# Issuing the NSA scores of a hybrid decoder layer inside the following dense product, one core of Trainium2

## The chip, the cores and the metric

One Trainium2 chip, one of its NeuronCores. The time is microseconds on the device for one execution of the whole layer. A run is compared by the median of its executions; the profile is of one further execution. The engines that matter here are TensorE (matmuls), VectorE, ScalarE and the queue of SyncE (SP), which issues the weight loads.

## What is computed

One decoder layer for 512 tokens of width 1024, in fp32. Three attention branches (MLA, a sparse attention "DSA", and NSA) run on one normed input, are gated and merged; cross-attention and an MLP follow. The change is in NSA, whose part of the reference is, shortened:

```python
p_c = masked_softmax(jnp.einsum('btghd,bcgd->bghtc', q, k_cmp) * scale, cmask)
o_c = jnp.einsum('bghtc,bcgd->btghd', p_c.astype(v_cmp.dtype), v_cmp)
...
s = jnp.einsum('btghd,bgtkd->bghtk', qb, kg) * scale + jnp.transpose(bias, (0, 1, 4, 2, 3))
p = masked_softmax(s, (dist >= 0)[:, :, None]).astype(vg.dtype)
o_s = jnp.einsum('bghtk,bgtkd->btghd', p, vg)
...
o = gt[:, :, 0] * o_c + gt[:, :, 1] * o_s + gt[:, :, 2] * o_w
```

There are 8 heads in 2 groups, 31 compressed keys, and, as every block is selected and the window spans the sequence, two causal attentions of 512 keys for each head (o_s and o_w, each with its own keys and values).

## The kernel before

The program gives each engine one list of instructions, and they meet through semaphores. Every list is in order, so a wait holds all that stands behind it on its engine.

**Dense products.** Weights come in slabs of 1 MB, numbered in one order. SP loads slab s into a raw buffer of two once slab s-2 has been split; ScalarE's `high(s)` copies it to its high part once the product that used that place (s-2) is done; VectorE's `low(s)` forms the low part. A product such as `features("nq", p)` is `t_mode` (L660 to L662 inside): 8 chunks of 6 matmuls of 512 columns, three for each of two output banks. `t_mode` calls a function `wait_chunk(k)` ahead of each chunk, where other work can be placed. Results stand in two PSUM pairs that alternate; `free(g)` waits for the one before the last to be taken.

**NSA by pairs.** The 8 heads are done in 4 pairs p. The slabs come in the order nq0, kk0, vv0, nq1, nq2, kk1, vv1, nq3 (nq: queries of a pair, kk and vv: keys and values of a group, two pairs each; compress weights lie between the first of them), and then bg20, bp20, bg21, bp21 and so on: branch gate and branch projection of the third merge. A pair has four causal units u = 2h + w (head h, kind w) and a compressed part for each head.

- Scores, TensorE (L773 in `score_tile`): 4 tiles a unit, of 128, 256, 384 and 512 columns, then two compressed tiles (L1035, four matmuls of 31 columns in each). They go through three PSUM buffers, `SCORE[n % 3]`; a tile waits until the tile three before it has been taken (`score_taken`). Two of these buffers also hold turned tiles, and one an output of the values.
- Softmax: VectorE adds the bias strip and finds the row maximum (`softmax_in`, L1893), ScalarE does the exp (`exps`, L1368), VectorE scales the row by gate over sum (`normalise`, L1904 to L1911). The compressed part has its own steps (L2055 to L2060, then L2071 to L2077).
- Values, TensorE: `attention` returns `begin(n)`, which turns the n-th block of probabilities (L783), and `finish()`, which runs value matmuls (L790), each followed by the turning two blocks on. ScalarE copies each turned block to SBUF (`turned_begin` for the first two, `turned` for the rest; the copy is L1268); a value matmul waits for its copy. At a head's end ScalarE and VectorE (`head_low`, L1916) take the output.

The order on TensorE in `block.tensor`: scores(0); product nq1; values(0); scores(1); product nq2; product kk1; values(1); product vv1; scores(2); product nq3; values(2); scores(3); product bg20; values(3); product bp20. `ahead(begin, KD)` places the first two turned blocks of the values in the last two chunks of the product before them. In `merge(2)` ScalarE applies the sigmoid (L1433) to bg20's result.

VectorE for a pair: takes all 16 score tiles, then the two compressed tiles, then one `low`, then the four `normalise`, then the compressed normalising. It does `low` for slab nq2 ahead of scores(0) and `head_low` of the pair before ahead of the scores. ScalarE for a pair: `turned_begin` of the last pair, query copy (`nsa_query`), `turned`, `high`, then four `exps` and the compressed exps; for pair 2 `high` stands ahead of `turned_begin`. POOL loads the next bias strips once all 18 score tiles of a pair are taken.

Of the kernel before, what the change touches and what calls it, by code (L numbers as in the profile page):

```python
# [81 lines left out]
def layer(nc, a, out):  # L82
# [11 lines left out]
    with ctx:  # L94
# [552 lines left out]
        def _(pe):  # L647
# [233 lines left out]
            def merge(b, last_values, after=lambda name, n: None):  # L881

                begin, finish = last_values
                for n in range(GROUPS):
                    g = product_at["bg", b, n]
                    free(g)
                    t_mode(slab_at["bg", b, n], two(g), both, KD, hT, None if n else ahead(begin, KD)).then_inc(product_ready, 1)
                    if n == 0:
                        finish()
# [93 lines left out]
            def nsa_values(p):  # L983
                heads = []
                for h in range(2):
                    parts = []
                    for w in range(2):
                        parts += causal_parts(16 + 6 * p + 2 * h + w, 2 * h + w, lambda j, w=w: vN[:, j, w * P:(w + 1) * P])
                    parts.append((16 + 6 * p + 4 + h, lambda i, h=h: probC[:, h, i, 0:NC], 0, NC, vcmp[0:NC, p // 2, :]))
                    heads.append((16 + 2 * p + h, parts))  # L990
                return attention(heads, 64 + 18 * p)
# [20 lines left out]
            for p in range(4):  # L1012
                r = p // 2
                if p:
                    begin, finish = nsa_values(p - 1)
                    features("nq", p, None if p == 2 else ahead(begin, KD))
                    if p == 2:
                        features("kk", r, ahead(begin, KD))
                    finish()
                    if p == 2:  # L1020
                        nsa_v(r)
                pe.wait_ge(taken["A"], taken_count[product_at["nq", p]])
                pe.wait_ge(taken["V"], taken_count[product_at["kk", r] if r else product_at["cmp"]])
                if p:
                    pe.wait_ge(attended_taken, 16 + 2 * p - 1)
                n = TILE_NSA + NSA_TILES * p
                for h in range(2):
                    for w in range(2):
                        for i in range(NT):
                            score_tile(n, [(qT[:, h, i * P:(i + 1) * P], kT[:, w, 0:(i + 1) * P])], (i + 1) * P)  # L1030
                            n += 1
                for h in range(2):
                    pe.wait_ge(score_taken, n - 2)
                    for i in range(NT):
                        mm = pe.matmul(SCORE[n % 3][:, i * 32:i * 32 + NC], qT[:, h, i * P:(i + 1) * P],  # L1035
                                       kcmpT[:, r * NC:(r + 1) * NC], start=True, stop=True)
                    mm.then_inc(score_ready, 1)
                    n += 1
                if p % 2 == 0:
                    pe.wait_ge(taken["A"], taken_count[product_at["vv", r]])  # L1040
            merge(2, nsa_values(3))


# [217 lines left out]
        def _(act):  # L1261
# [250 lines left out]
            nsa = 2 * causal + [(NC, T)]  # L1512
            for p in range(4):
                r = p // 2
                if p:
                    before = [(16 + 2 * (p - 1) + h, nsa) for h in range(2)]
                    if p != 2:
                        turned_begin(before, 64 + 18 * (p - 1))
                    nsa_query(p)
                    if p == 2:  # L1520
                        high(slab_at["nq", p] + 2)
                        turned_begin(before, 64 + 18 * (p - 1))
                    turned(before, 64 + 18 * (p - 1))
                    high(slab_at["kk", r] + 2 if p == 2 else slab_at["nq", p] + 2)
                if p == 2:
                    nsa_value(r)
                    high(slab_at["vv", r] + 2)
# [182 lines left out]
        def _(dve):  # L1710
# [317 lines left out]
            for p in range(4):  # L2028
                r = p // 2
                if p == 2:  # L2030
                    low(slab_at["nq", p] + 2)
                    nsa_key(r)
                if p == 0:
                    ready("hidT")
                    V.tensor_copy(hid[:, :, :, :].rearrange("p v k c -> p (v k c)"), bank("hidT")[:, 0, 0:8 * NC]).then_inc(taken["V"], 1)
                    ready("cmp")
                    V.tensor_copy(kcmpT[:, :], bank("cmp")[:, 0, 0:2 * NC])
# [5 lines left out]
                if p == 2:  # L2043
                    low(slab_at["kk", r] + 2)
# [314 lines left out]
```

## Time and profile before

| | |
|---|---|
| median of 3 runs | 1501.98 us (1501.86 to 1502.58) |
| the profiled execution | 1502.69 us |
| its span, first to last instruction | 1500.9 us |
| granted TensorE clock, mean | 0.997 of 2.4 GHz |
| TensorE busy | 1462.5 us, 97% |
| VectorE busy | 684.4 us, 46% |
| ScalarE busy | 569.8 us, 38% |
| chain that ended last | TensorE 94%, ScalarE 2%, VectorE 2% |

The work that the change touches lies between 655 and 850 us of the span. PE is TensorE, PEld its weight load, DVE VectorE, ACT ScalarE. A long matmul group's duration ends where its last matmul is modelled to end; since matmuls are pipelined, the time of one is read from start to start. An f32 matmul shows as two records.

### The profile page before, as it was taken

Reading aid. Unit: us, or ns where it says so; the run is one execution under the profiler, and the core shown is the slowest. Engines: PE = TensorE matmul, PEld = TensorE weight load, DVE = VectorE, ACT = ScalarE, POOL = GpSimd, SP = SyncE. Lnnn points to the kernel's source line nnn. Section 1 sums busy time; section 2 is a strip of 40 time slices with the busy share of each in tenths; the row PEclk is TensorE's granted clock in tenths of the full one; section 3 lists DMA queues with packets and bytes.
Section 4 is the critical chain, followed back from the end, with each engine's and each line's share of the span. In section 5 each row is a group of like instructions: output and inputs, shape, how many; then the busy total and the mean of one; then the engine's idle time right before and its main releaser. Section 6 shows DMA issues by size and latency. Waiting matters only on the chain.

```text
span 1500.9 us, 17329 instructions
## 1 busy us (share of the span) xinstructions
PE 1462.5 (97%) x7180; PEld 1178.6 (79%) x7180; DVE 684.4 (46%) x1186; ACT 569.8 (38%) x920; POOL 99.7 (7%) x74
## 2 busy tenths in 40 slices
PE   6999999999999999999999999999999999999998
PEld 5957777887877788876776788897778888888886
DVE  3566565764333355444554344483355332222334
ACT  4444543214333243445345423454344342223321
POOL 1000000022220001000000001000000220011100
PEclk9999999999999999999999999999999999999999
DMA  5211132232311334440210333254121323233321
GB/s 178 79 38 46 43 112 78 91 104 79 99 56 57 93 113 156 148 145 15 70 57 3 125 117 136 85 173 137 56 85 57 112 84 113 84 99 99 95 102 56
DMA packets 118270, 137.87 MB, mean 92 GB/s; under 512 B 7043, under 2 KB 98432, under 8 KB 118192
## 3 DMA queue, kind: packets, MB, share of 16 engines
q1 hardware_dynamic: 115200, 126.17, 26.6%
q0 software_dynamic: 2704, 10.00, 1.9%
q8 instruction: 57, 0.93, 0.3%
q10 hardware_dynamic: 288, 0.59, 0.1%
q14 instruction: 21, 0.17, 0.0%
HBM read 134.61 MB, written 2.14 MB: 91 GB/s over the span
## 4 chain that ended last, share of the span: by engine, by line
PE 94%; ACT 2%; DVE 2%; issue 1%; DMA 0%; SPq 0%; DVEq 0%; ACTq 0%
PE dense L660 25%; PE dense L662 25%; PE dense L661 25%; PE score L773 3%; PE turned L790 3%; PE score L790 3%; PE turned L773 2%; PE turned L783 1%; PE score L763 1%; PE score L783 1%; DVE probs L1893 1%; ACT probsT L1268 1%; PE score L1166 1%; PE score L1152 0%; PE turned L1152 0%
## 5 line engine op out<-in xcount | busy, mean ns | idle before, releaser
L1739 DVE TENSOR_TENSOR weight_low<-raw,weight_high 128x2048 fp32r<-128x2048 f32 (+2 forms) x96 | 201.2, 2102 | 375.0 <-ACT weight_high L1268 374.9
L660 PE MATMUL dense<-hidden_high,weight_high 128*128 128x512 f32 (+1 forms) x840 | 327.0, 389 | 4.0 <-ACT vN L1268 2.5
L662 PE MATMUL dense<-hidden_high,weight_low 128*128 128x512 f32 (+1 forms) x840 | 320.7, 382 | 0.0
L661 PE MATMUL dense<-hidden_low,weight_high 128*128 128x512 f32 (+1 forms) x840 | 320.2, 381 | 0.0
L1268 ACT ACTIVATE weight_high<-raw 128x2048 fp32r<-128x2048 f32 (+4 forms) x156 | 220.8, 1440 | 257.5 <-PE dense L662 255.0
L660 PEld LDWEIGHTS dense<-hidden_high,weight_high 128*128 128x128 f32 x840 | 158.0, 188 | 34.2 <-ACT vN L1268 2.9
L662 PEld LDWEIGHTS dense<-hidden_high,weight_low 128*128 128x128 f32 x840 | 157.9, 188 | 31.0
L661 PEld LDWEIGHTS dense<-hidden_low,weight_high 128*128 128x128 f32 x840 | 158.1, 188 | 29.7 <-issue 0.7
L1734 DVE TENSOR_TENSOR weight_low<-raw,weight_high 128x1024 fp32r<-128x1024 f32 x58 | 74.9, 1334 | 67.5 <-ACT weight_high L1268 67.5
L660 PE MATMUL dense<-weight_high,up_high 128*128 128x512 f32 x256 | 99.6, 389 | 0.0
L661 PE MATMUL dense<-weight_low,up_high 128*128 128x512 f32 x256 | 99.6, 389 | 0.0
L662 PE MATMUL dense<-weight_high,up_low 128*128 128x512 f32 x256 | 99.6, 389 | 0.0
L1368 ACT ACTIVATE probs<-probs,small 128x128 f32<-128x128 f32 (+3 forms) x128 | 70.3, 550 | 40.0 <-DVE small L1897 40.0
L660 PE MATMUL dense<-weight_high,hidden_high 128*128 128x256 f32 (+1 forms) x288 | 83.0, 288 | 0.0
L661 PE MATMUL dense<-weight_low,hidden_high 128*128 128x256 f32 (+1 forms) x288 | 81.5, 283 | 0.0
L662 PE MATMUL dense<-weight_high,hidden_low 128*128 128x256 f32 (+1 forms) x288 | 81.5, 283 | 0.0
L660 PE MATMUL dense<-branch_out_high,weight_high 128*128 128x512 f32 x192 | 75.1, 391 | 0.0
L662 PE MATMUL dense<-branch_out_high,weight_low 128*128 128x512 f32 x192 | 74.8, 389 | 0.0
L661 PE MATMUL dense<-branch_out_low,weight_high 128*128 128x512 f32 x192 | 74.7, 389 | 0.0
L773 PE MATMUL score<-kT,qT 128*128 128x128 f32 (+3 forms) x174 | 61.0, 452 | 4.7 <-DVE small L1893 2.5
L1268 ACT ACTIVATE probsT<-turned 128x512 f32<-128x512 f32 (+4 forms) x68 | 31.9, 470 | 87.7 <-PE turned L783 87.4
L1687 ACT ACTIVATE up<-dense 128x1024 f32<-128x1024 f32 x16 | 16.5, 1029 | 112.1 <-PE dense L662 112.1
(311 smaller groups left out, 2326.9 us busy)
## 6 DMA issues: line engine op xcount, KB each, us to landing
raw<-in_w_in SPq DMA_DIRECT2D x34, 1024.0 KB, 5.3
raw<-in_mlp_w SPq DMA_DIRECT2D x32, 1024.0 KB, 5.3
raw<-in_w_branch SPq DMA_DIRECT2D x12, 1024.0 KB, 5.1
raw<-in_nsa_cmp_w SPq DMA_DIRECT2D x8, 1024.0 KB, 5.3
raw<-in_cross_wkv SPq DMA_DIRECT2D x8, 1024.0 KB, 5.6
raw<-in_w_in SPq DMA_DIRECT2D x9, 512.0 KB, 5.1
bias_strips<-bias_scratch POOLq DMA_DIRECT2D x8, 512.0 KB, 4.1
raw<-in_w_out SPq DMA_DIRECT2D x4, 1024.0 KB, 5.1
```

What stands on the lines that cost most here:

```text
L660: pe.matmul(out_ap, ah, bh, start=first, stop=False)
L661: pe.matmul(out_ap, ah, bl, start=False, stop=False)
L662: return pe.matmul(out_ap, al, bh, start=False, stop=last)
L763: pe.matmul(S[n % 2][:, 0:(i + 1) * P], iqT[:, h // 2, i * P:(i + 1) * P], ikT[h % 2][:, 0:(i + 1) * P], start=True, stop=True).then_inc(i ...
L773: mm = pe.matmul(SCORE[n % 3][:, 0:cols], q, k, start=j == 0, stop=j == len(terms) - 1)
L783: mm = pe.transpose(TURNED[m % 2][0:rows, (i - i0) * P:(i - i0 + 1) * P], probs_of(i), ident[:, :])
L790: mm = pe.matmul(ATT[att % 2][:, i0 * P:T], value, probsT[0:rows, m % 3, 0:T - i0 * P], start=first, stop=last)
L1268: return nc.scalar.activation(dst, src, ACT.Copy, scale=scale)
L1368: ins = nc.scalar.activation(t, t, ACT.Exp, bias=negmax[:, k:k + 1], accum_out=total[:, k:k + 1])
L1687: nc.scalar.activation(h1[:, n % 2, :, :], bank(("up", f, n))[:, :, :], ACT.Relu).then_inc(taken["A"], 1)
L1734: V.tensor_tensor(dst, src, hi.bitcast(F32), ALU.subtract).then_inc(low_ready, 1)
L1739: ins = V.tensor_tensor(dst, src, hi.bitcast(F32), ALU.subtract)
```

## The change

TensorE: `nsa_scores(p)` gives a function that is called at each chunk of the next product. At chunk 0 it makes the waits that stood ahead of the scores and issues the two compressed tiles; the 16 causal tiles follow, 3 ahead of each of chunks 1 to 4 and 2 ahead of chunks 5 and 6. scores(0) stands inside nq1, scores(1) inside nq2, scores(2) inside nq3, scores(3) inside bg20. `nsa_turn` issues the first two turned blocks after the product (pairs 0, 2 and 3) or in the last chunk of kk1 (pair 1), and waits for all the scores to be taken. The compressed part of a head is turned between its two causal units.

VectorE: the compressed tiles are taken first; then unit 0, the compressed normalising, unit 1, normalise 0, unit 2, normalise 1, unit 3, a `low` (nq2 in pair 0, bg20 in pair 2), normalise 2 and 3, the `low` two slabs after the product's, and `head_low` for this pair. In pair 1, `nsa_key(1)` and `low` of nq3 stand ahead of `head_low`.

ScalarE: compressed exps, four exps, then `nsa_query(p + 1)`, `high`, `turned_begin`, `turned`. For pair 3, `turned_begin` stands behind the sigmoid. The number of matmuls, activations and vector operations is the same, and so is what is computed.

The diff, with removed loops cut to their first line:

```diff
@@ -878,14 +878,18 @@
 
             pe.wait_ge(taken["A"], taken_count[product_at["m4", 3]])
 
-            def merge(b, last_values, after=lambda name, n: None):
+            def merge(b, last_values, after=lambda name, n: None, last_scores=None):
 
                 begin, finish = last_values
                 for n in range(GROUPS):
                     g = product_at["bg", b, n]
                     free(g)
-                    t_mode(slab_at["bg", b, n], two(g), both, KD, hT, None if n else ahead(begin, KD)).then_inc(product_ready, 1)
+                    t_mode(slab_at["bg", b, n], two(g), both, KD, hT,
+                           None if n else last_scores or ahead(begin, KD)).then_inc(product_ready, 1)
                     if n == 0:
+                        if last_scores:
+                            nsa_turn(3, begin)
+                            pe.wait_ge(taken["A"], taken_count[product_at["vv", 1]])
                         finish()
                     after("bg", n)
                     g = product_at["bp", b, n]
@@ -985,8 +989,9 @@
                 for h in range(2):
                     parts = []
                     for w in range(2):
-                        parts += causal_parts(16 + 6 * p + 2 * h + w, 2 * h + w, lambda j, w=w: vN[:, j, w * P:(w + 1) * P])
-                    parts.append((16 + 6 * p + 4 + h, lambda i, h=h: probC[:, h, i, 0:NC], 0, NC, vcmp[0:NC, p // 2, :]))
+                        parts += causal_parts(16 + 6 * p + 2 + 2 * h + w, 2 * h + w, lambda j, w=w: vN[:, j, w * P:(w + 1) * P])
+                        if w == 0:
+                            parts.append((16 + 6 * p + h, lambda i, h=h: probC[:, h, i, 0:NC], 0, NC, vcmp[0:NC, p // 2, :]))
                     heads.append((16 + 2 * p + h, parts))
                 return attention(heads, 64 + 18 * p)
...
-            for p in range(4):
...
-            merge(2, nsa_values(3))
+            def compressed_score(p, h):
+
+                n = TILE_NSA + NSA_TILES * p + h
+                pe.wait_ge(score_taken, n - 2)
+                for i in range(NT):
+                    mm = pe.matmul(SCORE[n % 3][:, i * 32:i * 32 + NC], qT[:, h, i * P:(i + 1) * P],
+                                   kcmpT[:, p // 2 * NC:(p // 2 + 1) * NC], start=True, stop=True)
+                mm.then_inc(score_ready, 1)
+
+            def nsa_scores(p):
+
+                tiles = [(h, w, i) for h in range(2) for w in range(2) for i in range(NT)]
+                first = (0, 0, 3, 6, 9, 12, 14, 16, 16)
+
+                def at_chunk(k):
+                    if k == 0:
+                        pe.wait_ge(taken["A"], taken_count[product_at["nq", p]])
+                        pe.wait_ge(taken["V"], taken_count[product_at["kk", 1] if p > 1 else product_at["cmp"]])
+                        if p:
+                            pe.wait_ge(attended_taken, 16 + 2 * p - 1)
+                        for h in range(2):
+                            compressed_score(p, h)
+                    for m in range(first[k], first[k + 1]):
+                        h, w, i = tiles[m]
+                        score_tile(TILE_NSA + NSA_TILES * p + 2 + m,
+                                   [(qT[:, h, i * P:(i + 1) * P], kT[:, w, 0:(i + 1) * P])], (i + 1) * P)
+                return at_chunk
+
+            def nsa_turn(p, begin):
+
+                pe.wait_ge(score_taken, TILE_NSA + NSA_TILES * (p + 1))
+                begin(0)
+                begin(1)
+
+            for p in range(3):
+                begin, finish = nsa_values(p)
+                features("nq", p + 1, nsa_scores(p))
+                if p == 1:
+                    features("kk", 1, lambda k: nsa_turn(p, begin) if k == KD - 1 else None)
+                else:
+                    nsa_turn(p, begin)
+                pe.wait_ge(taken["A"], taken_count[product_at["vv", p // 2]])
+                finish()
+                if p == 1:
+                    nsa_v(1)
+            merge(2, nsa_values(3), last_scores=nsa_scores(3))
...
             def merge(b, tiles, first_tile):
                 heads = [(8 * b + 6 + h, tiles) for h in range(2)]
-                turned_begin(heads, first_tile)
+                if b < 2:
+                    turned_begin(heads, first_tile)
                 for n in range(GROUPS):
                     if b == 1 and n:
                         high(slab_at["bg", b, n] + 2)
@@ -1431,6 +1453,8 @@
                         last = product_at["bp", b, n - 1] if n else product_at["bp", b - 1, GROUPS - 1]
                         act.wait_ge(taken["V"], taken_count[last])
                     nc.scalar.activation(sig[:, :, :], bank(("bg", b, n))[:, :, :], ACT.Sigmoid).then_inc(taken["A"], 1)
+                    if n == 0 and b == 2:
+                        turned_begin(heads, first_tile)
                     if n == 0:
                         turned(heads, first_tile)
                     if b == 1 and n:
...
-            nsa = 2 * causal + [(NC, T)]
...
-                for u in range(4):
-                    exps(16 + 4 * p + u, u)
+            nsa = causal + [(NC, T)] + causal
+
+            def nsa_exps(p):
+
                 for h in range(2):
                     act.wait_ge(cmpmax_ready, 2 * p + h + 1)
                     t = probC[:, h, :, 0:NC]
                     nc.scalar.activation(t, t, ACT.Exp).then_inc(cmpexp_done, 1)
+                for u in range(4):
+                    exps(16 + 4 * p + u, u)
+
+            for p in range(3):
+                heads = [(16 + 2 * p + h, nsa) for h in range(2)]
+                nsa_exps(p)
+                nsa_query(p + 1)
+                high(slab_at["nq", p + 1] + 2)
+                turned_begin(heads, 64 + 18 * p)
+                turned(heads, 64 + 18 * p)
+                if p == 1:
+                    high(slab_at["kk", 1] + 2)
+                    nsa_value(1)
+                    high(slab_at["vv", 1] + 2)
+            nsa_exps(3)
             merge(2, nsa, 64 + 54)
...
-                n = TILE_NSA + NSA_TILES * p
-                dve.wait_ge(strips_loaded[p % 2], 16 * (p // 2 + 3))
...
+            def compressed_softmax(p):
+
                 for h in range(2):
-                    for w in range(2):
-                        softmax_in(n, 2 * h + w, lambda i, cols: strip_of(p, h, cols))
-                        n += NT
-                for h in range(2):
+                    n = TILE_NSA + NSA_TILES * p + h
                     dve.wait_ge(score_ready, n + 1)
...
-                    n += 1
-                    dve.wait_ge(score_taken, n)
+                    dve.wait_ge(score_taken, n + 1)
...
-                if p:
-                    low((slab_at["nq", p] if p % 2 else slab_at["vv", r]) + 2)
-                for h in range(2):
-                    for w in range(2):
-                        u = 2 * h + w
-                        c = (1 + w) * 8 + 2 * p + h
-                        normalise(16 + 4 * p + u, u, gateN[:, :, c])
+
+            def compressed_normalise(p):
+
                 for h in range(2):
                     dve.wait_ge(cmpexp_done, 2 * p + h + 1)
...
+
+            for p in range(4):
+
+                def unit_in(u):
+                    softmax_in(TILE_NSA + NSA_TILES * p + 2 + NT * u, u, lambda i, cols: strip_of(p, u // 2, cols))
+
+                def unit_out(u):
+                    c = (1 + u % 2) * 8 + 2 * p + u // 2
+                    normalise(16 + 4 * p + u, u, gateN[:, :, c])
+
+                dve.wait_ge(strips_loaded[p % 2], 16 * (p // 2 + 3))
+                compressed_softmax(p)
+                unit_in(0)
+                compressed_normalise(p)
+                unit_in(1)
+                unit_out(0)
+                unit_in(2)
+                unit_out(1)
+                unit_in(3)
+                if p == 0:
+                    low(slab_at["vv", 0] + 2)
+                elif p == 2:
+                    low(slab_at["vv", 1] + 2)
+                for u in range(2, 4):
+                    unit_out(u)
+                if p < 3:
+                    low(slab_at["nq", p + 1] + 2)
+                if p == 1:
+                    nsa_key(1)
+                    low(slab_at["kk", 1] + 2)
+                if p < 3:
+                    for h in range(2):
+                        head_low(16 + 2 * p + h)
             merge(2)
```

## Rows read from the trace of the kernel before

**Rows 1.** The page, busy us of each engine (share of the span) and instructions.

```profile
PE 1462.5 (97%) x7180; PEld 1178.6 (79%) x7180; DVE 684.4 (46%) x1186; ACT 569.8 (38%) x920; POOL 99.7 (7%) x74
```

**Rows 2.** Timeline of PE, pair 0: start, duration, line, out<-in, count [idle before <-releaser].

```profile
660.79 0.46 PE L773 MATMUL score<-kT,qT 128*128 128x128 f32 x2 [0.68 <-issue]
...
664.24 1.12 PE L773 MATMUL score<-kT,qT 128*128 128x512 f32 x2 [1.91 <-DVE small L1893]
...
675.14 1.06 PE L1035 MATMUL score<-k_cmpT,qT 128*128 128x31 f32 x8
...
687.85 1.02 PE L790 MATMUL score<-probsT,vN 128*128 128x512 f32 x2
```

**Rows 3.** Windows, 1 us each: PE, PEld, DVE, ACT, POOL, PEclk, DMA, GB/s.

```profile
666.00:667.00 1.00, 1.00 (x3) 0.55 (x3) 0.81 (x7) 0.66 (x3) 0.00 (x0) 0.50 1.14 344
...
668.00:669.00 1.00, 1.00 (x2) 0.34 (x1) 0.41 (x2) 0.63 (x2) 0.00 (x0) 0.50 0.99 240
```

**Rows 4.** Timeline of PE, first matmuls of product nq1; then six matmuls are one chunk.

```profile
676.03 0.48 PE L660 MATMUL dense<-hidden_high,weight_high 128*128 128x512 f32 x1
...
676.82 0.40 PE L660 MATMUL dense<-hidden_high,weight_high 128*128 128x512 f32 x1
...
678.18 0.39 PE L660 MATMUL dense<-hidden_high,weight_high 128*128 128x512 f32 x1
```

**Rows 5.** Timeline of PE, pairs 0 to 3: last value, first scores, first values.

```profile
703.69 1.12 PE L790 MATMUL turned<-probsT,v_cmp 31*128 31x512 f32 x2 [0.45 <-ACT probsT L1268]
704.74 0.49 PE L773 MATMUL score<-kT,qT 128*128 128x128 f32 x2
705.07 0.60 PE L773 MATMUL turned<-kT,qT 128*128 128x256 f32 x2
705.50 2.06 PE L773 MATMUL score<-kT,qT 128*128 128x384 f32 x4
...
739.50 1.02 PE L790 MATMUL score<-probsT,vN 128*128 128x512 f32 x2
...
768.00 0.39 PE L773 MATMUL score<-kT,qT 128*128 128x128 f32 x2
...
791.39 1.02 PE L790 MATMUL score<-probsT,vN 128*128 128x512 f32 x2
...
808.28 0.49 PE L773 MATMUL score<-kT,qT 128*128 128x128 f32 x2
...
832.16 1.02 PE L790 MATMUL score<-probsT,vN 128*128 128x512 f32 x2
```

**Rows 6.** Timeline of DVE, pair 0: last score tile, a normalise, the compressed normalising.

```profile
674.53 0.69 DVE L1893 CUSTOM_DVE_ANT_0 probs<-score,bias_strips 128x512 f32<-128x512 f32 x1 [0.29 <-PE score L773]
...
682.23 0.17 DVE L1904 RECIPROCAL small<-small 128x4 f32<-128x4 f32 x1
...
683.84 0.27 DVE L2071 TENSOR_REDUCE small<-cmp_probs 128x4 f32<-128x124 f32 x1
...
685.16 0.28 DVE L2071 TENSOR_REDUCE small<-cmp_probs 128x4 f32<-128x124 f32 x1
```

**Rows 7.** Timeline of ACT: exps of unit 3, a turned copy, query copy, high, sigmoid.

```profile
675.47 0.40 ACT L1368 ACTIVATE probs<-probs,small 128x128 f32<-128x128 f32 x1 [0.27 <-DVE small L1897]
...
677.67 0.49 ACT L1533 ACTIVATE cmp_probs<-cmp_probs 128x124 f32<-128x124 f32 x2
...
703.05 0.59 ACT L1268 ACTIVATE probsT<-score 31x512 f32<-31x512 f32 x1 [0.59 <-PE score L783]
...
727.98 1.03 ACT L1268 ACTIVATE qT<-dense 128x1024 f32<-128x1024 f32 x1 [9.06 <-PE dense L662]
728.90 1.91 ACT L1268 ACTIVATE weight_high<-raw 128x2048 fp32r<-128x2048 f32 x1
...
831.48 1.28 ACT L1433 ACT_TABLE_LOAD   x1
832.77 1.02 ACT L1433 ACTIVATE branch_gate<-dense 128x1024 f32<-128x1024 f32 x1
```

More of the change, by code:

```diff
@@ L1011, in _ @@
             compress()
-            for p in range(4):
-                r = p // 2
-                if p:
[L1015 to L1025, printed above, removed]
-                n = TILE_NSA + NSA_TILES * p
-                for h in range(2):
-                    for w in range(2):
-                        for i in range(NT):
-                            score_tile(n, [(qT[:, h, i * P:(i + 1) * P], kT[:, w, 0:(i + 1) * P])], (i + 1) * P)
-                            n += 1
-                for h in range(2):
[L1033 to L1040, printed above, removed]
@@ L1511, in _ @@
                 high(slab_at[(name, *i) if name == "cw" else (name, i)] + 2)
-            nsa = 2 * causal + [(NC, T)]
[L1513 to L1527, printed above, removed]
-                for u in range(4):
-                    exps(16 + 4 * p + u, u)
+            nsa = causal + [(NC, T)] + causal
+            def nsa_exps(p):
                 for h in range(2):
@@ L2027, in _ @@
             dve.wait_ge(gates_ready, 1)
[L2028 to L2037, printed above, removed]
-                    V.tensor_copy(vcmp[0:NC, :, :], bank("cmp")[0:NC, 1, 0:2 * P].rearrange("p (r c) -> p r c", c=P)).then_inc(taken["V"], 1)
-                    low(slab_at["vv", 0] + 2)
-                if p:
-                    for h in range(2):
-                        head_low(16 + 2 * (p - 1) + h)
-                if p == 2:
-                    low(slab_at["kk", r] + 2)
-                n = TILE_NSA + NSA_TILES * p
-                dve.wait_ge(strips_loaded[p % 2], 16 * (p // 2 + 3))
+            ready("hidT")
+            V.tensor_copy(hid[:, :, :, :].rearrange("p v k c -> p (v k c)"), bank("hidT")[:, 0, 0:8 * NC]).then_inc(taken["V"], 1)
+            ready("cmp")
+            V.tensor_copy(kcmpT[:, :], bank("cmp")[:, 0, 0:2 * NC])
+            V.tensor_copy(vcmp[0:NC, :, :], bank("cmp")[0:NC, 1, 0:2 * P].rearrange("p (r c) -> p r c", c=P)).then_inc(taken["V"], 1)
+            def compressed_softmax(p):
                 for h in range(2):
-                    for w in range(2):
-                        softmax_in(n, 2 * h + w, lambda i, cols: strip_of(p, h, cols))
-                        n += NT
-                for h in range(2):
+                    n = TILE_NSA + NSA_TILES * p + h
                     dve.wait_ge(score_ready, n + 1)
@@ L2055, in _ @@
                     V.tensor_tensor(t, SCORE[n % 3][:, 0:P].rearrange("p (t c) -> p t c", c=32)[:, :, 0:NC], late[:, :, :], ALU.add).then_inc(score_taken, 1)
-                    n += 1
-                    dve.wait_ge(score_taken, n)
+                    dve.wait_ge(score_taken, n + 1)
                     link(V.tensor_reduce(m, t, AX, ALU.max))
@@ L2060, in _ @@
                     V.tensor_tensor(t, t, m.unsqueeze(2).broadcast_to((P, NT, NC)), ALU.subtract).then_inc(cmpmax_ready, 1)
-                if p:
-                    low((slab_at["nq", p] if p % 2 else slab_at["vv", r]) + 2)
-                for h in range(2):
-                    for w in range(2):
-                        u = 2 * h + w
-                        c = (1 + w) * 8 + 2 * p + h
-                        normalise(16 + 4 * p + u, u, gateN[:, :, c])
+            def compressed_normalise(p):
                 for h in range(2):
```

## Prediction

> **What bounds the kernel now.** I read the page's busy line first: TensorE is busy for 97% of the span [rows 1], so time can only come from its own order of work or from the few gaps in it. The changed code runs between 660.8 and 849 us, four pairs of NSA heads one after the other, so I then followed TensorE alone through that stretch in the timeline, and after it VectorE and ScalarE beside it.
>
> Each pair has a phase of scores and a phase of values, with dense products between. I measure from the first score matmul to the first value matmul:
> - pair 0: 660.79 to 687.85, 27.06 us. It holds a wait of 1.91 us on VectorE, which is splitting a weight slab [rows 2], and behind that wait the granted clock falls to half (1.2 GHz) for three whole microseconds [rows 3], which costs some 1.5 us.
> - pair 1: 704.74 to 739.50, 34.76 us (two products in it)
> - pair 2: 768.00 to 791.39, 23.39 us
> - pair 3: 808.28 to 832.16, 23.88 us [rows 5]
>
> Pairs 2 and 3 show what the scores cost there: 23.39 and 23.88 less a product with its two turned tiles, 11.82 (676.03 to 687.85) [rows 2, 4], leaves 11.6 and 12.1 us. The matmuls themselves need 10.8 of these (below). So at most about 1 us a pair can be won by placing scores better; they are work of the engine that is already full, and putting them "inside" a product hides none of it. What counts is the waits won and the waits made.
>
> **The scores inside the product.** Costs on TensorE: a chunk of a product is six matmuls, 676.82 to 678.18, 1.36 us, a product eight of them, 10.9 us [rows 4]. A score tile of 128 columns takes 0.33 us (704.74 to 705.07), one of 256 takes 0.43 (705.07 to 705.50) [rows 5]; by that rate 384 take 0.65 and 512 take 0.86, together 2.27 us a unit, 9.1 us for four. A head's compressed scores take about 0.85 [rows 2], 1.7 for both. Going from the product to f32 matmuls and back: product 10.9 and two turned tiles 0.75 (0.43 and 0.32, by the same rate) leave 0.17 of the 11.82 for two trips, 0.08 each. The change makes seven trips a product. Without any wait the new product takes 10.9 + 9.1 + 1.7 + 0.55 = 22.3 us.
>
> Now the waits. There are three score buffers, so tile m is held until VectorE has taken tile m-3. VectorE's new order puts `compressed_normalise`, 2.64 us (twice 1.32, 683.84 to 685.16), between unit 0 and unit 1, and `unit_out`, 1.61 us (682.23 to 683.84), before units 2 and 3 [rows 6]. I set both queues beside each other, with T = 0 at the first compressed score. TensorE has issued tile 3 (the last of unit 0) by 6.85. VectorE takes it until 7.9, normalises until 10.5, takes tile 4 at 10.7. TensorE has tiles 4, 5 and 6 out by 9.70 and waits for tile 4 until 10.8: 1.1 us. `unit_out(0)` then runs from 12.65 to 14.25, and TensorE's tile 11 meets it with no real wait. The last score tile ends at 20.5, the product at 23.3. So a pair's scores cost 23.3 - 10.9 = 12.4 us in place of 11.6 to 12.1. Nothing is won there.
>
> **What stands behind the product.** This is the step that decides. In the kernel before, the first two probability tiles are turned in the last two chunks of the product, and their copy by ScalarE is covered by dense matmuls. After the change `nsa_turn` issues them only behind the product (pairs 0 and 2), and ScalarE's order ahead of `turned_begin` is: the four exps of unit 3, the query copy `nsa_query`, and a whole slab's `high`. Four exps take 2.20 us (675.47 to 677.67) and start 0.94 us after VectorE takes up the last tile (674.53 to 675.47) [rows 6, 7]: 20.7 + 0.94 + 2.20 = 23.9. The query copy holds ScalarE for 0.92 (727.98 to 728.90), `high` for 1.91, the first copy of a turned tile for 0.59, and its value matmul follows it at once (703.05 to 703.69) [rows 5, 7]. 23.9 + 0.92 + 1.91 + 0.60 = 27.3. TensorE is done with both turned tiles at 24.1, so it stands for 3.2 us. The slab that this `high` splits is first needed behind the values, over 16 us later; here it only stands in the way.
>
> - pair 0: 27.3 against 27.06, +0.3. The old wait of 1.91 and its slow clock go, the new wait of 3.2 and most likely the same slow clock come.
> - pair 1: here a second product (`kk`) covers query copy and `high`, and the tiles are turned before its last chunk: 23.3 + 10.9 + 0.75 + 0.1 = 35.1 against 34.76, +0.3.
> - pair 2: 27.3 against 23.39, +3.9.
> - pair 3: the product is the branch gate's. ScalarE now does the sigmoid before `turned_begin`, where it did it behind. The function table is loaded straight behind the last work of the engine, without waiting for the sigmoid's input (831.48, 1.28 us, ahead of the activation at 832.77) [rows 7], but now that is behind the exps: 23.9 + 1.28 + 0.92 + 0.60 = 26.7 against 23.88, +2.8.
>
> The page "ScalarE: Activation LUTs" of the Trainium skill, section "What ACT_TABLE_LOAD costs", gives a switch of table 1.28 us for the load and some 1.38 us more for a drain. By that pair 3 would lose 1.4 us more and the sum would end at 1510.9. The rows show no drain outside the load: I keep the 1.28.
>
> **The values.** In the old order the compressed part stands last, and the second head's last value waits 0.45 us on ScalarE (at 703.69) [rows 5]; then the step from a 31-row matmul to a full one costs 0.19 (703.69 + 0.86 = 704.55 to 704.74). In the new order the compressed part stands between two causal units. The 0.45 shrinks to the 0.2 or so that a copy leaves open inside the chain, and the 0.19 behind the last value goes: -0.5 a pair, -2.0 for four.
>
> **The clock.** The trace has one fall, behind 1.91 us of standing still [rows 2, 3]. Pairs 2 and 3 get new waits of 3.2 and 2.6 us, where nothing fell before. A fall costs up to 1.6 us; bounds 0 and 1.6 each. Part of a fall can lie inside the wait itself, and the values' chain has gaps that absorb some: I take 1.0 each, 2.0 in all.
>
> **Moved and without cost.** VectorE's `low` for slabs nq2, bg20 (2.3 us each) move between unit 3's scores and unit 2's normalising: unit 2 is turned about 8 us after the first value matmul, so there are over 8 us of cover. The `low` of bp20 comes a pair earlier, so SP's loads behind it only get earlier. SP's load of vv1 waits for `low` of nq2, now at about 684 instead of 664: its slab is first needed behind pair 1's values, past 755. POOL's strip loads wait for the pair's last score, now 5 to 8 us later, with a pair's time of cover. `nsa_key(1)` waits for the `kk` product on VectorE with `low` of nq3 and two `head_low` behind it; the value matmuls of pair 1 wait only for heads of pair 0, and the next product but one needs nq3.
>
> **Sum.** 0.3 + 0.3 + 3.9 + 2.8 - 2.0 + 2.0 = +7.3 us. The profiled execution took 1502.69 (span 1500.9, 1.8 around it), so 1510.0 for such a one; it lies 0.7 above the median of 1501.98, from which I get 1509.3.
>
> **Rivals.**
> 1. No fall of the clock in the new waits, and none in pair 0 either: 7.3 - 2.0 - 1.5 = +3.8, 1505.8. For it: a gap can fall so that it harms nothing. Against it: 1.91 us were enough once.
> 2. Each trip between product and scores is dearer. The only step between kinds of matmul that shows a price is 0.19 [rows 5]. At 0.2 a trip instead of 0.08 it is 28 x 0.12 = 3.4 more, 1512.7. Two such trips in the old product cost 0.17 together, which speaks against it.
> 3. The scores do fit: loads of the 128-column tiles hide behind dense matmuls (0.12 x 4), trips are free (0.55), VectorE is never late (1.1), about 2.1 a pair, 8.5 in all. With the slow clock that is 7.3 - 8.5 = -1.2, 1500.8, no measurable change.
> 4. Faster, the other side: the scores fit as in 3, and the clock doesn't fall as in 1: 3.8 - 8.5 = -4.7, 1497.3. It decides from where VectorE frees tile 4 before TensorE has issued tile 6, that is, from a `compressed_normalise` under about 1.5 us; the rows show 2.64.
> 5. That the change doesn't do what it says is part of my forecast: "values directly behind" holds for TensorE's list alone, while ScalarE has 3 us of other work queued there.
>
> **Chances.** Forecast (own range 1507 to 1512) 0.52, rival 1 0.23, rival 2 0.10, rival 3 0.08, rival 4 0.07. The range 1502 to 1514 holds the first three, 0.85, with an error of each of them. A measurement of this kernel can tell about 0.2%, 3.0 us, from no change. Slower by more than that are the forecast, rival 2 and most of rival 1, 0.78; within it rival 3 and the rest of rival 1, 0.15; faster 0.07.
>
> **What would show it.** In the profile after: a wait of some 3 us of the first value matmul on ScalarE behind the products nq1 and nq3, of 2.6 behind bg20, none behind kk1; a wait of about 1 us of a score tile on VectorE in the fourth chunk of each product; half clock behind two or three of these waits; a score product of 23.3 us; no 1.91 us wait at 662. I am wrong if score products end near 21 us, or if the first value matmul follows the product within 1 us, or if the clock stays full.

## The result: 11 us slower, and the profile after

The changed kernel takes 1513.27 us (median of 4 runs, 1511.77 to 1514.77) against 1502.23 (1501.86 to 1502.58): ratio 1.0074, 95% interval 1.0056 to 1.0091. On a second chip it took 1513.77 against 1501.75 (1.0079, interval 1.0064 to 1.0094). The forecast was 1509.3 and slower, its range ended at 1514. The direction and the places were right, the size was 3.7 us too small, and the narrower range that went with the forecast alone, 1507 to 1512, was missed.

The page of the changed kernel has the same work in it as [rows 1], 17329 instructions, but a span of 1512.9 us in place of 1500.9:

```profile
PE 1466.4 (97%) x7180; PEld 1181.9 (78%) x7180; DVE 684.7 (45%) x1186; ACT 569.7 (38%) x920; POOL 99.8 (7%) x74
```

Where the time went is seen in one view, the waits of TensorE in the changed stretch, 655 to 870 us (us in total, times, longest):

```profile
PE score L790 <- issue: 6.1, 2, 3.0
PE score L773 <- DVE small L1918: 4.7, 4, 1.2
PE score L790 <- ACT branch_gate L1455: 2.7, 1, 2.7
PE score L1022 <- DVE v_cmp L2057: 0.8, 1, 0.8
```

Two waits of 3.0 us and one of 2.7 ahead of a value matmul (L790), and four of 1.2 at a score tile (L773). The first two are put down to "issue"; that they are ScalarE's is read from its own timeline, pair 0:

```profile
684.36 0.41 ACT L1389 ACTIVATE probs<-probs,small 128x128 f32<-128x128 f32 x1 [2.65 <-DVE small L1922]
...
686.56 1.00 ACT L1289 ACTIVATE qT<-dense 128x1024 f32<-128x1024 f32 x1
687.47 1.90 ACT L1289 ACTIVATE weight_high<-raw 128x2048 fp32r<-128x2048 f32 x1
689.27 0.58 ACT L1289 ACTIVATE probsT<-turned 128x512 f32<-128x512 f32 x1
```

The exps of unit 3, the query copy, the slab's high part and only then the first turned tile stand without a gap. In pair 3 the function table and the sigmoid stand there instead:

```profile
840.45 1.28 ACT L1455 ACT_TABLE_LOAD   x1
841.75 1.02 ACT L1455 ACTIVATE branch_gate<-dense 128x1024 f32<-128x1024 f32 x1
842.67 0.59 ACT L1289 ACTIVATE probsT<-turned 128x512 f32<-128x512 f32 x1
```

TensorE's side, pairs 0, 1, 2 and 3, from the first compressed score to the first value matmul:

```profile
660.99 1.05 PE L1022 MATMUL score<-k_cmpT,qT 128*128 128x31 f32 x8 [0.84 <-DVE v_cmp L2057]
...
673.38 1.13 PE L773 MATMUL score<-kT,qT 128*128 128x512 f32 x2 [1.17 <-DVE small L1918]
...
689.94 2.05 PE L790 MATMUL score<-probsT,vN 128*128 128x512 f32 x2 [3.03 <-issue]
...
707.98 1.04 PE L1022 MATMUL score<-k_cmpT,qT 128*128 128x31 f32 x8
...
743.03 1.02 PE L790 MATMUL score<-probsT,vN 128*128 128x512 f32 x2
...
770.85 0.97 PE L1022 MATMUL score<-k_cmpT,qT 128*128 128x31 f32 x8
...
794.19 0.60 PE L783 MATMUL turned<-ident,probs 128*128 128x128 f32 x4
...
798.15 1.12 PE L790 MATMUL score<-probsT,vN 128*128 128x512 f32 x2 [3.03 <-issue]
...
816.37 1.05 PE L1022 MATMUL score<-k_cmpT,qT 128*128 128x31 f32 x8
...
843.36 1.94 PE L790 MATMUL score<-probsT,vN 128*128 128x512 f32 x2 [2.66 <-ACT branch_gate L1455]
```

| pair | first score to first value, before [rows 2, 5] | forecast | after | first value to next pair's first score, before | after |
|---|---|---|---|---|---|
| 0 | 27.06 | 27.3 | 28.95 | 16.89 | 18.04 |
| 1 | 34.76 | 35.1 | 35.05 | 28.50 | 27.82 |
| 2 | 23.39 | 27.3 | 27.30 | 16.89 | 18.22 |
| 3 | 23.88 | 26.7 | 26.99 | | |

(Pair 1's last columns hold product vv1 too.) The differences add up to 11.0 us; 0.2 lie ahead of pair 0 and the rest of the 12.0 us between the two spans behind pair 3's first value. In pair 2 the product with the scores takes 23.34 us (770.85 to 794.19), 23.3 by the forecast.

The granted clock in single microseconds (columns as in [rows 3]):

```profile
663.00:664.00 1.00, 1.00 (x4) 0.81 (x5) 0.93 (x4) 0.31 (x1) 0.00 (x0) 0.50 0.00 0
...
690.00:691.00 1.00, 1.00 (x2) 0.48 (x3) 1.00 (x1) 0.22 (x1) 0.00 (x0) 0.50 1.19 294
...
800.00:801.00 1.00, 1.00 (x4) 0.45 (x3) 0.12 (x1) 0.12 (x1) 0.00 (x0) 0.50 0.00 0
...
844.00:845.00 1.00, 1.00 (x2) 0.23 (x1) 0.00 (x0) 0.00 (x0) 0.00 (x0) 0.50 0.00 0
```

Four times half clock in this stretch, three of them at the end of the new waits, where [rows 3] shows one. (Both profiles also have some 3 us at half clock near 21 us of the span, far ahead of the change.) What these cost, and what the rest costs, the profile doesn't separate; the runs do.

### The profile page after: what moved, and what is told of

It is laid out like the page before. It is cut to its first block, busy times and chain, and to the rows that moved or that the text cites. A ratio compares the mean times of both kernels' runs of the same rounds, so it can differ in the third digit from the quotient of the medians.

```text
span 1512.9 us, 17329 instructions
## 1 busy us (share of the span) xinstructions
PE 1466.4 (97%) x7180; PEld 1181.9 (78%) x7180; DVE 684.7 (45%) x1186; ACT 569.7 (38%) x920; POOL 99.8 (7%) x74
## 4 chain that ended last, share of the span: by engine, by line
PE 92%; DVE 3%; ACT 2%; issue 1%; DMA 0%; SPq 0%; DVEq 0%; ACTq 0%
PE dense L660 25%; PE dense L662 25%; PE dense L661 24%; PE score L773 3%; PE turned L790 3%; PE score L790 3%; PE turned L773 2%; PE turned L783 1%; PE score L763 1%; PE score L783 1%; DVE probs L1918 1%; PE score L1187 1%; ACT probs L1389 1%; ACT probsT L1289 0%; PE score L1173 0%
## 5 line engine op out<-in xcount | busy, mean ns | idle before, releaser
L660 PE MATMUL dense<-hidden_high,weight_high 128*128 128x512 f32 (+1 forms) x840 | 333.3, 397 | 4.0 <-ACT vN L1289 2.5
L773 PE MATMUL score<-kT,qT 128*128 128x128 f32 (+3 forms) x174 | 57.9, 436 | 5.6 <-DVE small L1918 5.3
```

What stands on the lines that cost most here:

```text
L660: pe.matmul(out_ap, ah, bh, start=first, stop=False)
L773: mm = pe.matmul(SCORE[n % 3][:, 0:cols], q, k, start=j == 0, stop=j == len(terms) - 1)
```

## The experiments

Two theories at first. A: ScalarE's order makes the waits behind the product, and standing still makes the clock fall. B: the interleaving itself carries the loss. Each is compared with the kernel before on the same chip. after_again, scalar_order, late_cnorm and filled_wait ran on one chip, order_fixed, order_late, turn_inside and before_filled on another, inside_low and values_order on a third; the kernel before took 1501.75, 1501.79 and 1501.87 us there. The changed kernel was measured on the first of the three, 1513.77, so differences to it from the other two go across chips.

**The changed kernel once more.**

> The changed kernel once more, with profiles. Two groups of times were seen, 1511.8 and 1514.7 us. Theory A (the clock): the 2.9 us between them are one or two falls of TensorE's clock that happen in one execution and not in another, so each new time lies near one of the two values and a profiled execution at 1511.8 shows two windows of half clock or fewer where the one at 1514.77 shows four (at 663, 690, 800 and 844 us). Theory B (something other, as loads that land late): the number of windows at half clock is the same at both times, and some wait differs.

1513.77 us. Its profiled execution (1513.83) has three falls of the clock (stretches at half clock) in the changed stretch, near 665, 692 and 842, and the same waits to 0.1 us. The one of pair 2 is missing, and there the values take 16.38 us in place of 18.22. So the number of falls differs from execution to execution of one program, and the waits don't. No profile fell on an execution at 1511.8, so that these have fewer falls is supported by their mean clock alone (0.997 against 0.993 to 0.996), which also counts falls far from the change. Falls aren't all that differs: the first score stands at 662.07 here and at 660.99 in the first profile, in code that is the same.

**The waits filled with matmuls.** Work is added whose results are overwritten.

> The changed kernel with 13 extra matmuls of 512 columns on data at hand behind the turned tiles of pairs 0 and 2 and 11 in pair 3, whose results are overwritten: they fill the waits of 3.0, 3.0 and 2.7 us without shortening them. Theory A (standing still makes the clock fall): no half clock behind these three waits, the values phases take 16.1 us instead of 17.9 as in pair 1, 5.1 us less in all, about 1508.2 us. Rival C (the half clock comes at other times or costs nothing, the waits alone carry the loss): within 1 us of the changed kernel, or longer if the filling overruns the wait.

```diff
                 begin(0)
                 begin(1)
+                if p != 1:
+                    pe.wait_ge(attended_taken, 16 + 2 * p)
+                    for _ in range(13 if p < 3 else 11):
+                        pe.matmul(OT, hTH[:, 0, 0:P], hTH[:, 0, :], start=True, stop=True)
```

1509.41 us (1508.65 to 1510.38), 4.4 less than the changed kernel; ratio to before 1.0053, interval 1.0038 to 1.0068. TensorE's timeline:

```profile
686.73 3.23 PE L1053 MATMUL turned<-hidden_high 128*128 128x512 f32 x13
690.00 1.10 PE L790 MATMUL score<-probsT,vN 128*128 128x512 f32 x2
...
706.39 1.04 PE L1022 MATMUL score<-k_cmpT,qT 128*128 128x31 f32 x8
```

The filling takes the place of the wait, the first value matmul comes no earlier behind it, and the values of pair 0 take 16.39 us (690.00 to 706.39) in place of 18.04. No window behind the three waits is below full clock. A kernel that does more work is faster, so standing still brings the fall about: rival C is out. By the profiles a fall behind a wait costs 1.65 us (18.04 against 16.39, pair 0) to 1.84 (18.22 against 16.38, pair 2). 5.1 us were expected and 4.4 came; the repeated profile has only two of the three falls.

**VectorE's order alone.**

> VectorE alone reordered: compressed_normalise behind unit 3's scores instead of between unit 0 and unit 1 (the order in which the probabilities count is changed with it). Theory A: the wait of 1.2 us of a score tile in each of the four products goes, the products and the exps behind them end 1.1 us earlier, 4.4 us less in all, about 1508.9 us, with the 3.0 us waits on ScalarE and the half clock unchanged. Rival B (VectorE and TensorE are out of step by design, the wait only moves to a later tile): less than 2 us gained, 1511 or more.

```diff
                 unit_in(0)
-                compressed_normalise(p)
                 unit_in(1)
                 unit_out(0)
                 unit_in(2)
                 unit_out(1)
                 unit_in(3)
+                compressed_normalise(p)
```

1506.85 us (1504.19 to 1507.27), ratio 1.0031, interval 1.0018 to 1.0044. The waits of TensorE in the stretch:

```profile
PE score L790 <- issue: 6.1, 2, 3.0
PE score L790 <- ACT branch_gate L1455: 2.7, 1, 2.7
PE score L1022 <- DVE v_cmp L2057: 0.8, 1, 0.8
```

The row of four times 1.2 is gone, the others stand. 4.4 us were expected and 6.9 came. Fewer falls don't explain the rest: in the stretch this profile has the same three as that of after_again (near 663, 690 and 837, none in pair 2), and the mean clock of its executions is no higher (0.994 to 0.997 against 0.995 to 0.997). From first score to first value the pairs take 27.47, 33.60, 25.84 and 25.51 us, 1.5 less each than in after_again, 5.9 in all. So a score tile's wait of 1.2 us costs 1.5, for a reason that wasn't looked for. Another 1.3 us of the difference between the two profiles lie ahead of the stretch, in code that is the same.

**ScalarE's order alone, and what I had overlooked.**

> ScalarE alone reordered, in pairs 0 and 2: turned_begin, query copy, turned, and high last; pairs 1 and 3 as in the changed kernel. Theory A (ScalarE's order makes the wait, and the wait makes the clock fall): the first value matmul of pairs 0 and 2 comes 2.8 us earlier (exps end, 0.6 us of copy), no wait over 0.5 us there, no half clock behind it, 1.7 us each: 9.0 us less than the changed kernel, 1503 to 1505.5 us. Rival B (the score tiles inside the product carry the loss, through switching and VectorE's waits): at most 1 us less, 1511 or more. Rival C (the wait goes, but the clock has nothing to do with it): 5.6 us less, about 1507.5.

```diff
-                nsa_query(p + 1)
-                high(slab_at["nq", p + 1] + 2)
+                if p == 1:
+                    nsa_query(p + 1)
+                    high(slab_at["nq", p + 1] + 2)
                 turned_begin(heads, 64 + 18 * p)
+                if p != 1:
+                    nsa_query(p + 1)
                 turned(heads, 64 + 18 * p)
+                if p != 1:
+                    high(slab_at["nq", p + 1] + 2)
```

1525.44 us, ratio 1.0158 (1.0143 to 1.0173): 12 us slower than the changed kernel, where all three expectations had it faster or the same. The first value matmul did come early, but look what follows (PE, then DVE):

```profile
686.42 1.10 PE L790 MATMUL score<-probsT,vN 128*128 128x512 f32 x2 [0.40 <-issue]
...
708.58 1.88 PE L1022 MATMUL score<-k_cmpT,qT 128*128 128x31 f32 x8 [5.61 <-DVE branch_out_low L1946]
```

```profile
705.43 2.29 DVE L1769 TENSOR_TENSOR weight_low<-raw,weight_high 128x2048 fp32r<-128x2048 f32 x1 [16.60 <-ACT weight_high L1289]
707.64 0.68 DVE L1946 TENSOR_TENSOR branch_out_low<-score,branch_out_high 128x512 fp32r<-128x512 f32 x1
```

The wait of 3.0 became 0.4. But VectorE's `low` for that slab stands ahead of `head_low`. With `high` behind the values, VectorE stood 16.6 us at `low` with `head_low` queued behind it, and the next pair's scores wait for `head_low`: 5.6 and 5.8 us of standing still, before pairs 1 and 3. In each of these waits the clock fell, and it stayed at half for over 10 us (about 706 to 716 in pair 1). So the `high` that I called "only in the way" could not be moved by itself.

**Both sides of that chain moved.**

> The kernel scalar_order left TensorE standing 5.6 us in front of the next pair, because head_low stands behind low of slab kk1 on VectorE, and that low now waited for the late high. Here ScalarE has the same order (turned tiles first, high behind the values; in pair 3 the sigmoid behind the values too), and VectorE's low of that slab moves into the next pair, behind unit 3's scores. Theory A (ScalarE's order makes the wait, the clock falls behind it, and scalar_order failed only by what queued behind low): the first value matmul of pairs 0, 2 and 3 comes 24.5 us after the first score (27.3 and 27.0 before this edit), no half clock behind it; 12 us less than the changed kernel: 1500.5 us, within 2 of the kernel before. Rival B (the interleaved product loses by itself): 1506 or more.

ScalarE's part is that of scalar_order, and in pair 3 the sigmoid stands behind the values. VectorE's part:

```diff
                 unit_in(3)
                 if p == 0:
                     low(slab_at["vv", 0] + 2)
                 elif p == 2:
                     low(slab_at["vv", 1] + 2)
+                else:
+                    low(slab_at["nq", p] + 2)
...
-                if p < 3:
-                    low(slab_at["nq", p + 1] + 2)
```

1503.24 us (1501.57 to 1503.93), ratio 1.0011 (1.0001 to 1.0021): 10.5 us less than the changed kernel, 12 were expected (1500.5 us), rival B wanted 1506 or more. First score to first value, pair 2:

```profile
766.03 0.97 PE L1022 MATMUL score<-k_cmpT,qT 128*128 128x31 f32 x8
...
790.69 1.10 PE L790 MATMUL score<-probsT,vN 128*128 128x512 f32 x2 [0.41 <-issue]
```

24.66 us in place of 27.30 (24.69 and 24.72 in pairs 0 and 3), and no window of the stretch is below full clock. This profile is of the quickest of ten executions, though, 1.7 us below the median; whether the usual one has full clock there isn't shown. Rival B is out: with all scores still inside the products the loss is some 1.5 us. Most of it came from ScalarE's order and the clock behind it. What is left of it can be seen in pair 2, 24.66 us against 23.39 before: VectorE's wait is still there, and the turned tiles still stand behind the product.

**Both orders.**

> order_fixed and late_cnorm together. Theory A: the gains add, as each product ends 1.1 us earlier and the exps behind it too: 4.4 us less than order_fixed, 1496 us, faster than the kernel before by 6. Rival: once the waits on ScalarE are gone, exps(3) or VectorE takes their place and less than 2 us of the 4.4 come through, 1499 or more.

1501.90 us, ratio 1.000 (0.9991 to 1.0010), 1.3 less and not 4.4. The rival was right: VectorE took the waits' place, but through a weight slab and not through the scores. The product nq2 now ends before VectorE, busy with the compressed normalising, has split the next slab:

```profile
727.27 0.77 PE L660 MATMUL dense<-hidden_high,weight_high 128*128 128x512 f32 x1 [3.19 <-DVE weight_low L1768]
```

3.19 us in pair 1, where order_fixed had 0.53, and half clock behind it (727 to 731). Pairs 2 and 3 did gain their 1.5 us each (23.22 and 23.24 in place of 24.66 and 24.72); pair 1 lost 2.7.

**The turned tiles back under the product, then the slab's low part ahead.**

> order_late with the score tiles one chunk earlier and the first two turned tiles of pairs 0, 2 and 3 in the last chunk of the product, as in the kernel before. Theory A: the copies of the turned tiles are covered by dense matmuls; the first value matmul comes 0.4 to 0.6 us earlier in three pairs: 1.5 us less than order_late. Rival: the earlier tiles meet VectorE in the compressed softmax and wait there, and the gain is 0 or a loss of up to 2.

Against order_late, shortened:

```diff
-                first = (0, 0, 3, 6, 9, 12, 14, 16, 16)
+                first = (0, 3, 6, 9, 12, 14, 16, 16, 16)
...
+                    if begin and k == KD - 1:
+                        nsa_turn(p, begin)
```

1497.98 us, ratio 0.9981 (0.9969 to 0.9994), 3.9 less than order_late where 1.5 were expected (one of its ten executions took 1506.35 us at a mean clock of 0.946, the others 1496.2 to 1499.2). The wait for kk1's low part shrank to 1.8 us without half clock behind it, which I had not foreseen: by the profiles pair 1 gave 2.4 us and the three pairs of the theory 0.5, 0.4 and 0.1.

> turn_inside left one wait of 1.8 us, of product kk1 for its low part, which VectorE does behind the compressed normalising in pair 1. Here that low stands ahead of the compressed normalising in pair 1. Theory A: the wait falls to under 0.3 us and nothing takes its place, because the values of pair 1 come a whole product later: 1.6 to 1.8 us less than turn_inside, 1496.3 us, some 5.5 less than the kernel before. Rival: the normalised probabilities come late for the turned tiles of pair 1 and the wait moves there, no change.

Against turn_inside:

```diff
                 unit_in(3)
+                if p == 1:
+                    low(slab_at["nq", 1] + 2)
                 compressed_normalise(p)
```

1495.39 us (1494.74 to 1496.23), ratio 0.9957, interval 0.9944 to 0.9971: 6.5 us faster than the kernel before, 18 faster than the change and 2.6 than turn_inside, where 1.6 to 1.8 were expected. One wait is left in the stretch, and half clock behind it (663 to 667):

```profile
PE score L1021 <- DVE v_cmp L2061: 0.8, 1, 0.8
```

From first score to first value the pairs take 24.36, 34.01, 22.75 and 23.14 us.

**The values' order alone, on the kernel before.**

> The kernel before with one part of the change alone: the compressed part of a head is turned and multiplied between its two causal units. Theory A (the term of the forecast): the wait of 0.45 us of the last value matmul of each pair and the step of 0.19 behind it go, 0.5 us a pair, 2.0 us less than the kernel before in all. Rival: the new place opens gaps of its own and less than 1 us comes through, which a measurement can't tell from none.

```diff
                     for w in range(2):
                         parts += causal_parts(16 + 6 * p + 2 * h + w, ...)
-                    parts.append((16 + 6 * p + 4 + h, ...))
+                        if w == 0:
+                            parts.append((16 + 6 * p + 4 + h, ...))
...
-            nsa = 2 * causal + [(NC, T)]
+            nsa = causal + [(NC, T)] + causal
```

1499.57 us (1498.80 to 1501.03), ratio 0.9985 (0.9976 to 0.9994), 2.3 less; 2.0 were expected. Pair 0:

```profile
661.27 0.46 PE L773 MATMUL score<-kT,qT 128*128 128x128 f32 x2 [0.68 <-issue]
...
664.71 1.13 PE L773 MATMUL score<-kT,qT 128*128 128x512 f32 x2 [1.91 <-DVE small L1894]
...
686.88 1.02 PE L790 MATMUL score<-probsT,vN 128*128 128x512 f32 x2
...
703.20 0.39 PE L773 MATMUL score<-kT,qT 128*128 128x128 f32 x2
```

The values take 16.32 us in place of 16.89. And, though the wait of 1.91 us is there, this execution has no half clock: the phase ahead takes 25.61 us, not 27.06.

**The old wait filled.**

> The kernel before with 8 extra matmuls (results overwritten) in the wait of 1.91 us of pair 0. Theory A (standing still makes the clock fall, and a fall costs 1.5 us there): no half clock near 666 us, 1.3 to 1.6 us less than the kernel before, about 1500.5. Rival (the clock falls here for another reason, as the compress stage ahead of it): the half clock stays and the time is the same.

1501.58 us (1499.95 to 1502.41), ratio 0.9997 (0.9987 to 1.0006). In the profile the wait is gone from the list, there is no half clock, and pair 0 takes 25.63 us from first score to first value in place of 27.06. But the median is only 0.2 us lower where 1.3 to 1.6 were expected, and the interval (2.0 less to 0.9 more) holds both the expectation and no change: this run doesn't decide. One explanation is that the old fall isn't in every execution. values_order shows that the wait of 1.91 us can pass without a fall, and of the 55 executions of the kernel before on the three chips 30 have a mean clock of 0.999, that of this profile without half clock, where the profiled one of [rows 3] has 0.997. The mean clock doesn't say where a fall is, and the profiled one has another near 21 us. So that the old fall is missing in most executions is likely, and not shown.

## Why the prediction was right in direction and short in size

**What bounds the kernel, and that scores inside a product hide nothing:** right. The score tile's wait in the fourth chunk was 1.2 us where 1.1 was forecast, and late_cnorm shows it is VectorE's order. That the product took the forecast 23.3 us is in part luck: without the wait it takes 21.88 (pair 2 of late_cnorm, 767.64 to 789.52) and not 22.3, and the wait costs 1.5 and not 1.1, two errors of 0.4 that cancel.

**What stands behind the product:** right, to 0.1 us in pair 2 and 0.3 in pair 3 (26.99 against 26.7). The four things in ScalarE's queue stand in the trace as they were added up. The rule of the Trainium skill (page "ScalarE: Activation LUTs", "What ACT_TABLE_LOAD costs") would, as an estimate, have put pair 3 at 28.1 (26.7 and its drain of 1.38). The trace has 26.99, and no drain beside the load (840.45 to 841.73, the sigmoid at 841.75). Its sum would have been 1510.7 and not the 1510.9 that the forecast gives.

**The values:** right. -2.0 was the term, -2.3 the measured one.

**The clock: mis-sized, and it is the term that failed, in four ways.** 
- I took 1.0 a fall because part of it might lie in the wait or in gaps. The profiles have 1.65 and 1.84; filling the three waits gave back 4.4 us in the medians, 1.5 each if all three are usual.
- The sum has 2.0 for the falls of pairs 2 and 3 and nothing for the new one of pair 0. I set it against the old one, but the two don't stand in the same place: the old one is inside the 27.06 us from first score to first value, the new one begins behind them, in the values, and the 27.3 don't hold it. The term should have had three falls. So 4.4 where the sum had 2.0.
- I counted the old fall as always paid, from a single profiled execution. Without it the old phase takes 25.61 us, and the change costs 27.3 - 25.6 = 1.7 there and not 0.3. How often it is paid stays open (before_filled).
- A fall that I had not forecast at all stands inside pair 0's product (663 us), behind the 0.84 us ahead of its first score. With it pair 0 took 28.95 us in both the changed kernel and filled_wait (661.05 to 690.00), where 27.3 were forecast: some 1.6 us.

Put together, the old fall taken as missing and all new ones as present: 1.7 + 1.6 + 0.3 + 3.9 + 3.1 - 2.3 + 4.4 = 12.7 us; 12.0 were measured on the second chip, 11.0 on the first. Without the three falls behind the waits it is 8.3, and filled_wait lost 7.7. Against the forecast's 7.3 the three falls have 2.4 more, the fall in pair 0 1.6, the old fall 1.4, pair 3 0.3, the values 0.3 less. The sum is 0.7 to 1.7 too large. Executions of one program spread over 3 us, and two profiles of it differ by a fall and by 1.1 us ahead of the stretch. How often each fall comes was not measured, so the terms of the clock are sizes where a fall comes, and this remainder stays open.

**The rivals.** Rival 1 (no fall) is out: three of the new waits have one in the first profile. Rival 2 (dear trips) is out: the product is 23.34 us long. Rivals 3 and 4 needed a VectorE that frees tile 4 in time. late_cnorm gave that, and TensorE still stood behind the product; the gain is only there once ScalarE's order, VectorE's `low` and the place of the turned tiles go with it (inside_low). Rival 5 was the case.

**One sentence was wrong beside the sum:** that the `high` "only stands in the way". It also feeds the `low` that `head_low` waits behind. As a description of the change it cost nothing; as advice it cost 12 us in scalar_order.

## What to carry to other kernels

When work is moved under other work of the same full engine, look at what used to be covered there: here two small turned tiles lost their cover, and ScalarE's list had 3 us ahead of their copies. Before an instruction is moved on one engine, follow its product into every other in-order queue and name what stands behind the consumer there. A stop of TensorE of 2.7 us or more was mostly paid a second time in clock here; whether a fall seen in one profile belongs to the kernel's usual time has to be asked of several executions.

## What the hardware showed that I had not expected

- A wait of 2.7 to 3.2 us was followed by some 3 us at half clock in nine cases of eleven (after, after_again, late_cnorm, scalar_order, order_late). Those of 5.6 and 5.8 us (scalar_order) came with over 10 us of it. One of 1.9 us (kernel before) was followed by half clock in one profile and by none in another (values_order), one of 1.8 (turn_inside) by none. The waits of 1.2 us at a score tile were never followed by it (20 of them, in five profiles).
- At the start of the interleaved product, behind a gap of only 0.84 us, the clock fell too (between 661 and 669 us), in eight of the nine profiles of kernels with the scores inside; order_fixed has none. What decides this was not tried.
- A function table is loaded directly behind the engine's last work, ahead of the wait of the activation that needs it: in the changed kernel at 661.71, behind a slab's high part, while the exp that needs it waits for VectorE until 663.31.
